# Product-key experts on one core: five dense token tiles and three gathered, with whole expert rows fetched

## The chip, the core and the metric

The kernel runs on one core of a Trainium2 chip. Its engines are TensorE (PE), VectorE (DVE), ScalarE (ACT), GpSimd (POOL) and SyncE (SP), which here only issues transfers. The metric is the time of one execution on the device in microseconds, the median of several runs.

## What is computed

One decoder layer over 1024 tokens of width 1024: normalisation, a joint projection, sliding-window and forgetting attention, a gated mix, and then the part that matters here, a product-key expert layer with 16384 experts. For each token eight heads choose 16 experts each, 128 in all:

```python
idx = jnp.take_along_axis(cidx, pos, axis=-1)         # (T, 8, 16)
g = jax.nn.softmax(top, axis=-1).astype(xc.dtype)
u = expert_down[idx]
act = jax.nn.gelu(jnp.einsum('td,thkd->thk', xc, u), approximate=False)
vv = expert_up[idx]
return jnp.einsum('thk,thkd->td', g * act, vv)
```

A last normalisation follows.

## The kernel before

The stages run one after the other: norm, projections, attention, mixing, output and second norm, `routing`, `gate_table`, `experts`. The 1024 tokens are eight tiles of 128. Every float32 product is made of three matmuls (high x high, high x low, low x high), so each weight is split by ACT (a copy, `hi`) and by DVE or POOL (a subtract, `lo`).

The expert layer is computed in two ways. For the first `DT` = 6 tiles (`SD` = 768 tokens) it is *dense*: all 16384 experts, as 128 blocks of 128, are multiplied with all tokens, and a table of gates (zero where an expert wasn't chosen) masks the result. The other two tiles (`GTILES`) are *gathered*: for each of the 128 choices ("slots") of each of these tiles an indirect DMA on POOL's queue fetches one row for each of 128 tokens. 256 slots x 2 (once the down row, once the up row) are 512 fetches of 4 KB rows, 0.5 MB each.

The down product of a dense block (gelu(down x h), L1347 to L1349 and L403 to L405) needs no gate, so it is spread over three stages: 28 blocks "ahead" in `routing`, three a head; 48 (`AHEAD_TABLE`) in `gate_table`, one a step; the other 52 (`FRESH`) in `experts`. Blocks done ahead are stored to DRAM and loaded again. Each runs in two halves of 512 and 256 tokens (`dense_cols`).

`gate_table` has 48 steps of four groups of four tokens (`GS`, `GT`). DVE builds one-hot vectors (L1869, L1873, L1890), ACT a fourth (L1943), PE multiplies them (L1830, L1831), ACT drains the group. After every four steps SP stores 4 MB of table; the load of the down block for the next step but two stands behind it in SP's queue. In between, two slots a step get their dot product on DVE (L1880, 96 in all, `TABLE_SLOTS`), from a ring of three rows.

`experts` walks over 128 chunks `c` (one expert block each). A chunk loads the up block, the gates and, if fresh, the down block, otherwise the stored gelus. DVE multiplies gate and gelu (`gate`, L2293), ACT and POOL split the weight (L2245, L2443) and the up block (L2241, L2450). PE adds up three chunks at a time (`SPAN`) for each group of 128 tokens x 512 columns (`up`, L2211 to L2213): 12 groups, four `visits` a chunk, over six PSUM banks; DVE adds each finished group to `acc` in SBUF (`add`, L2301). Between these, DVE handles the slots: first the dots of the rest of the down rows (L2308, 160), with a gelu of ACT for each 16 and a weight, then the up rows, each scaled and added to `acc` in SBUF (L2319, 256). They are dealt out by `share`, four for a fresh chunk and one for another. POOL fetches them into a ring of five rows; a fetch waits until DVE has used the buffer's last row (L2434). At the end the residual is added, the norm made and the result stored.

All order within an engine is written out by hand; engines wait for each other by semaphores.

Of the kernel before, what the change touches and what calls it, by code (L numbers as in the profile page):

```python
# [40 lines left out]
QW = 256  # L41
DT = 6
SD = DT * P
GTILES = TT - DT
# [65 lines left out]
def cols_of(x, k, h):  # L110

    return x[:, 2 * h:2 * h + 2, k]
# [1185 lines left out]
class Ahead:  # L1298


    def __init__(self, nc, m, t, a, name, first, count, raw=None, landed=None, stored=None):
        self.nc, self.m, self.t, self.a = nc, m, t, a
        self.first, self.count = first, count
        self.raw = m.at(name + "downT", [P, 2, KT, P], 172) if raw is None else raw
        self.hi = m.at(name + "downT_hi", [P, 2, KT, P], 180, F32R)
        self.lo = [m.at(name + "downT_lo0", [P, KT, P], 188, F32R), m.at(name + "downT_lo1", [P, KT, P], 15, F32R)]
# [59 lines left out]
AHEAD_TABLE = 48  # L1366
AHEAD = AHEAD_ROUTING + AHEAD_TABLE
FRESH = N_CHUNKS - AHEAD
TABLE_SLOTS = 96
# [5 lines left out]
def routing(nc, m, t, a):  # L1375
# [3 lines left out]
    ah = Ahead(nc, m, t, a, "ra_", 0, AHEAD_ROUTING, t.ra_raw, t.ra_landed)  # L1379
# [374 lines left out]
def gate_table(nc, m, t, a):  # L1754
# [3 lines left out]
    ah = Ahead(nc, m, t, a, "ga_", AHEAD_ROUTING, AHEAD_TABLE, stored=t.ga_stored)  # L1758
# [8 lines left out]
    g_hi = m.at("g_hi", [P, SD], 157, F32R)  # L1767
    g_lo = m.at("g_lo", [P, SD], 160, F32R)
    DEEP = 3
    ROWS = 3  # L1770
    LEAD = 2
    hot = [m.at(f"g_hot{i}", [P, 3, GT, P], kb, F32R) for i, kb in enumerate((192, 198, 44))]
    hot1 = [m.at(f"g_hot1_{i}", [P, GT, P], kb, BF16) for i, kb in enumerate((204, 205, 50))]
    row = [m.at(f"g_row{i}", [P, D], kb) for i, kb in enumerate((76, 80, 3))]
    r_land = [m.sem(f"g_row_landed{i}") for i in range(ROWS)]
    r_used = m.sem("g_row_used")
# [23 lines left out]
    with nc.Block() as block:  # L1800
        @block.tensor
        def _(pe):
# [8 lines left out]
            for w in range(GTILES):  # L1811
                if w:
                    pe.wait_ge(rows_copied, 2 * w)
                for k in range(KT):
                    out = m.psum[:, 2 + k // 4, (k % 4) * P:(k % 4 + 1) * P]
                    for part, x in enumerate((t.hT_hi, t.hT_lo)):
                        mm = nc.tensor.matmul(out, x[:, SD // QW, k, w * P:(w + 1) * P].bitcast(F32), t.ident[:],
                                              start=part == 0, stop=part == 1)
# [30 lines left out]
        def _(dve):  # L1849
            for x in range(6):  # L1850
                c, h = divmod(x, NH)
                dve.wait_ge(turned, x + 1)
                mine = dense_cols(h)
# [23 lines left out]
            def slot(s):  # L1877
                r = s % ROWS
                dve.wait_ge(r_land[r], (s // ROWS + 1) * 16)
                nc.vector.scalar_tensor_tensor(out=row[r][:], in0=row[r][:], scalar=1.0, in1=t.hrows[:, s // P],  # L1880
                                               op0=ALU.mult, op1=ALU.mult,
                                               accum_out=t.first_dots[:, s:s + 1]).then_inc(r_used, 1)

            def step(n, u):
                mine = range(TABLE_SLOTS * n // STEPS, TABLE_SLOTS * (n + 1) // STEPS)
                for y in range(GS):
# [6 lines left out]
                    if y == 2:  # L1893
                        ah.rest_v(dve, n + 1, 1 - u)
# [738 lines left out]
```

## Time and profile before

| | |
|---|---|
| median of 3 runs | 3502.55 us (3501.09 to 3503.83) |
| span of the profiled execution | 3503.6 us |
| PE busy | 3309.6 us, 94% |
| DVE busy | 2510.1 us, 72% |
| POOL busy | 1725.2 us, 49% |
| ACT busy | 1203.9 us, 34% |
| moved by DMA | 668.76 MB, 191 GB/s on the mean |

The profiled execution is one run, its span 1.05 us above the median of the timed ones. "L" numbers are lines of the kernel before. PE's busy time overlaps within itself (matmuls are pipelined), so its pace is read from the starts of matmuls. DMA share is the mean busy share of the core's 16 DMA engines; it can pass 1 slightly in short windows. Stages, by the first work of each: `routing` from about 970 us, `gate_table` from 1352, `experts` from 1968.

### The profile page before, as it was taken

What the parts mean: (1) busy time and instruction counts of PE and PEld (TensorE: products, weight loads), DVE (VectorE), ACT (ScalarE), POOL (GpSimd) and SP (SyncE); (2) the same over time, 40 slices, a digit from 0 to 9 for tenths busy, and PEclk for the clock granted to TensorE, in tenths of its full rate; (3) what the DMA queues carried; (4) which work ended last, traced back from release to release, by engine and by line L of the source; (5) the groups of instructions that cost most, each with busy time, mean ns of one, the idle gap of its engine ahead of it and who ended that gap; (6) DMA issues with size and microseconds to landing.
All of it is one profiled execution on the core that took longest, in us unless ns stands there. A gap on an engine that the chain in (4) does not pass through costs nothing.

```text
span 3503.6 us, 49480 instructions
## 1 busy us (share of the span) xinstructions
PE 3309.6 (94%) x17307; PEld 2817.1 (80%) x17307; DVE 2510.1 (72%) x5042; ACT 1203.9 (34%) x2314; POOL 1725.2 (49%) x1037
## 2 busy tenths in 40 slices
PE   5999988988899998999999799999999999999997
PEld 4888767777778877988888688888888888888885
DVE  5111056642469998888889588888888888888888
ACT  3111145542222223676667422222222222222222
POOL 2992000014034443111111378767877788778776
PEclk9999989999999998999999899999999999999998
DMA  5443210024222223666676688888888888888886
GB/s 205 126 128 118 72 49 13 13 91 150 78 71 92 71 69 112 251 222 243 248 255 229 250 273 265 275 253 269 273 269 268 256 274 270 273 257 264 274 260 206
DMA packets 406649, 668.76 MB, mean 191 GB/s; under 512 B 217936, under 2 KB 269208, under 8 KB 403616
## 3 DMA queue, kind: packets, MB, share of 16 engines
q1 hardware_dynamic: 325472, 371.35, 33.1%
q0 software_dynamic: 78656, 286.30, 24.9%
q10 hardware_dynamic: 2304, 8.39, 0.6%
q8 instruction: 116, 1.90, 0.2%
q14 instruction: 101, 0.83, 0.1%
HBM read 567.35 MB, written 97.55 MB: 190 GB/s over the span
## 4 chain that ended last, share of the span: by engine, by line
PE 50%; DMA 5%; DVE 5%; ACT 1%; issue 1%; SPq 0%; POOL 0%; DVEq 0%; ACTq 0%
PE psum L2211 10%; PE psum L2212 10%; PE psum L2213 10%; DMA ga_downT<-in_expert_downT 5%; PE psum L405 4%; PE psum L404 4%; PE psum L403 4%; PE psum L1347 2%; PE psum L1349 2%; PE psum L1348 2%; PE psum L1831 1%; PE psum L1830 1%; DVE g_hot L1869 1%; DVE g_hot L1890 1%; DVE g_hot L1873 1%; DVE g_row L1880 1%
## 5 line engine op out<-in xcount | busy, mean ns | idle before, releaser
L2211 PE MATMUL psum<-e_u_hi,e_w_hi 128*128 128x512 f32 x1536 | 600.0, 391 | 22.3 <-POOL e_u_lo L2450 18.6
L2212 PE MATMUL psum<-e_u_lo,e_w_hi 128*128 128x512 f32 x1536 | 599.5, 390 | 0.0
L2213 PE MATMUL psum<-e_u_hi,e_w_lo 128*128 128x512 f32 x1536 | 598.9, 390 | 0.0
L2319 DVE SCALAR_TENSOR_TENSOR acc<-e_row,e_row_weights,acc 128x1024 f32<-128x1024 f32 x256 | 481.1, 1879 | 20.4 <-DMA e_row<-in_expert_up,rows_of 12.5
L2301 DVE TENSOR_TENSOR acc<-acc,psum 128x512 f32<-128x512 f32 x508 | 337.0, 680 | 158.4 <-PE psum L2213 152.4
L2450 POOL TENSOR_TENSOR e_u_lo<-e_up,e_u_hi 128x1024 fp32r<-128x1024 f32 x128 | 385.2, 3009 | 72.1 <-ACT e_u_hi L2241 71.5
L2437 POOL DMA_INDIRECT e_row<-in_expert_up,rows_of x256 | 330.4, 1290 | 65.8 <-issue 53.4
L2211 PEld LDWEIGHTS psum<-e_u_hi,e_w_hi 128*128 128x128 f32 x1536 | 289.5, 188 | 81.8 <-issue 19.0
L2241 ACT ACTIVATE e_u_hi<-e_up 128x1024 fp32r<-128x1024 f32 x128 | 135.9, 1062 | 630.0 <-DMA e_up<-in_expert_up 410.0
L1909 POOL DMA_INDIRECT g_row<-in_expert_down,rows_of x96 | 110.8, 1154 | 485.4 <-DVE g_row L1880 467.6
L2213 PEld LDWEIGHTS psum<-e_u_hi,e_w_lo 128*128 128x128 f32 x1536 | 289.1, 188 | 60.6
L2212 PEld LDWEIGHTS psum<-e_u_lo,e_w_hi 128*128 128x128 f32 x1536 | 289.5, 189 | 58.2
L2443 POOL TENSOR_TENSOR e_w_lo<-e_table,e_w_hi 128x768 fp32r<-128x768 f32 x128 | 249.0, 1945 | 163.7 <-ACT e_w_hi L2245 162.7
L2308 DVE SCALAR_TENSOR_TENSOR e_row<-e_row,h_rows 128x1024 f32<-128x1024 f32 x160 | 275.0, 1738 | 17.2 <-DMA e_row<-in_expert_down,rows_of 17.1
L1347 PE MATMUL psum<-hT_hi,ga_downT_hi 128*128 128x512 f32 (+1 forms) x768 | 272.6, 355 | 3.7 <-DVE ga_downT_lo L1339 3.7
L405 PE MATMUL psum<-hT_hi,e_downT_lo 128*128 128x256 f32 (+1 forms) x816 | 274.2, 336 | 0.0
L404 PE MATMUL psum<-hT_lo,e_downT_hi 128*128 128x256 f32 (+1 forms) x816 | 274.2, 336 | 0.0
L403 PE MATMUL psum<-hT_hi,e_downT_hi 128*128 128x256 f32 (+1 forms) x816 | 273.9, 336 | 0.0
L495 DVE TENSOR_TENSOR pw_lo<-pw_raw,pw_hi 128x1024 fp32r<-128x1024 f32 (+1 forms) x33 | 45.5, 1378 | 316.8 <-ACT pw_hi L461 316.8
L1943 ACT ACTIVATE g_hot<-g_hot,g_lo 128x128 fp32r<-128x128 bf16 x768 | 244.5, 391 | 64.1 <-DVE g_hot L1869 61.3
L1349 PE MATMUL psum<-hT_hi,ga_downT_lo 128*128 128x512 f32 (+1 forms) x768 | 262.5, 342 | 0.0
L1348 PE MATMUL psum<-hT_lo,ga_downT_hi 128*128 128x512 f32 (+1 forms) x768 | 261.7, 341 | 0.0
(290 smaller groups left out, 7834.0 us busy)
## 6 DMA issues: line engine op xcount, KB each, us to landing
e_up<-in_expert_up SPq DMA_DIRECT2D x128, 512.0 KB
e_table<-gate_table SPq DMA_DIRECT2D x128, 384.0 KB
gate_table<-g_table SPq DMA_DIRECT2D x11, 4096.0 KB, 15.0
e_left<-gelus_ahead SPq DMA_DIRECT2D x76, 384.0 KB
e_left<-in_expert_downT SPq DMA_DIRECT2D x51, 512.0 KB
ga_downT<-in_expert_downT SPq DMA_DIRECT2D x49, 512.0 KB
gelus_ahead<-ga_gelu SPq DMA_DIRECT2D x48, 384.0 KB, 3.5
pw_raw<-in_w_in SPq DMA_DIRECT2D x34, 512.0 KB, 3.8
```

Of the source, the lines that this page charges most:

```text
L403: nc.tensor.matmul(out, l_hi(k), r_hi(k), start=k == 0, stop=False)
L404: nc.tensor.matmul(out, l_hi(k), r_lo(k), start=False, stop=False)
L405: mm = nc.tensor.matmul(out, l_lo(k), r_hi(k), start=False, stop=k == steps - 1)
L1347: mm(out, self.hi[:, u, k], dense_of(self.t.hT_hi, k, h), start=k == 0, stop=False)
L1348: mm(out, self.hi[:, u, k], dense_of(self.t.hT_lo, k, h), start=False, stop=False)
L1349: return mm(out, self.lo[u][:, k], dense_of(self.t.hT_hi, k, h), start=False, stop=k == KT - 1)
L2211: nc.tensor.matmul(to, W_hi[:, q, rows], U_hi[:, q, cols], start=c == mine[0], stop=False)
L2212: nc.tensor.matmul(to, W_hi[:, q, rows], U_lo[:, q, cols], start=False, stop=False)
L2213: mm = nc.tensor.matmul(to, W_lo[:, q, rows], U_hi[:, q, cols], start=False, stop=c == mine[-1])
L2301: nc.vector.tensor_tensor(group(j), group(j), m.psum[:, 2 + J % BANKS], ALU.add).then_inc(acc_d, 1)
L2319: nc.vector.scalar_tensor_tensor(out=mine, in0=ring[r][:], scalar=weights[:, k:k + 1], in1=mine, op0=ALU.mult, op1=ALU.add).then_inc(r_use ...
L2450: nc.gpsimd.tensor_tensor(U_lo[:, c % WRING], Uraw[:, c % 2], U_hi[:, c % WRING].bitcast(F32), ALU.subtract).then_inc(u_lo, 1)
```

## The change

Five tiles are dense (640 tokens, halves of 384 and 256) and three gathered. The tokens' tile in `hT` is 128 wide in place of 256, with high and low side by side. A new input holds for each expert its down row and its up row next to each other; a slot is one indirect DMA of 8 KB rows, 1 MB. DVE takes the dot with the first half (`dot`), ACT makes gelu and weight of this one slot (`row_weight`, two activations of 128 x 1), and DVE adds the second half, scaled, to a sum that stays in two PSUM banks for a whole tile (`add_row`), one slot later; ACT copies the sum to `acc` at the end of a tile. There are 384 slots, 40 of them in `gate_table` (one a step; that stage now has 40 steps, so 60 blocks are fresh), 344 in `experts`. The rings hold two and four 8 KB rows. The banks for groups are four; the ten groups are visited 3, 3 and 4 in turn. A fetch waits until the row sum of the slot that had its buffer is made.

```diff
-QW = 256
-DT = 6
+QW = 128
+DT = 5
 SD = DT * P
+HALVES = (0, -(-DT // 2) * P, SD)
 GTILES = TT - DT
...
 def dense_of(x, k, h):
-    return x[:, 2 * h:min(2 * h + 2, SD // QW), k]
+    return x[:, HALVES[h] // QW:HALVES[h + 1] // QW, k]

 def dense_cols(h):
-    return slice(h * HALF, min((h + 1) * HALF, SD))
+    return slice(HALVES[h], HALVES[h + 1])
...
-AHEAD_TABLE = 48
+AHEAD_TABLE = 40
...
-TABLE_SLOTS = 96
+TABLE_SLOTS = 40
+SLOTS = GTILES * P
...
-    ROWS = 3
+    ROWS = 2
...
-            def slot(s):
+            def dot(s):
                 r = s % ROWS
                 dve.wait_ge(r_land[r], (s // ROWS + 1) * 16)
-                nc.vector.scalar_tensor_tensor(out=row[r][:], in0=row[r][:], scalar=1.0, in1=t.hrows[:, s // P],
-                                               op0=ALU.mult, op1=ALU.mult,
-                                               accum_out=t.first_dots[:, s:s + 1]).then_inc(r_used, 1)
+                nc.vector.scalar_tensor_tensor(out=row[r][:, 0:D], in0=row[r][:, 0:D], scalar=1.0,
+                                               in1=t.hrows[:, s // P], op0=ALU.mult, op1=ALU.mult,
+                                               accum_out=t.dots[:, s:s + 1]).then_inc(r_dot, 1)
...
-                    for x, s in enumerate(mine):
-                        if x == y or y == GS - 1 and x > y:
-                            slot(s)
+                    if y == 1 and n < TABLE_SLOTS:
+                        dot(n)
...
+                    if y == 3 and n < TABLE_SLOTS:
+                        add_row(n)
...
             def fetch(s):
-                if s >= TABLE_SLOTS:
-                    return
-                at_least(pool, r_used, s - ROWS + 1)
-                nc.gpsimd.indirect_dma_start(out=row[s % ROWS][:], out_offset=None, in_=a.expert_down[0],
+                at_least(pool, r_acc, s - ROWS + 1)
+                nc.gpsimd.indirect_dma_start(out=row[s % ROWS][:], out_offset=None, in_=a.expert_rows,
...
-    BANKS = 6
-    RING = 5
-    SLOTS = GTILES * P
+    BANKS = 4
+    RING = 4
...
-    share = [4 if is_fresh(c) else 1 for c in range(NG)]
-    HERE = 2 * SLOTS - TABLE_SLOTS
+    share = [3 if is_fresh(c) else 1 for c in range(NG)]
+    HERE = SLOTS - TABLE_SLOTS
...
-                    to = m.psum[:, 2 + J % BANKS]
+                    to = m.psum[:, 4 + J % BANKS]
...
-            def row_gelu(e):
-                act.wait_ge(r_used, (e + 1) * TOPK - TABLE_SLOTS)
-                mine = slice(e * TOPK, (e + 1) * TOPK)
-                nc.scalar.activation(dots[:, mine], dots[:, mine], ACT.Gelu).then_inc(r_gelu, 1)
+            def row_weight(s):
+                mine = t.dots[:, s:s + 1]
+                act.wait_ge(r_dot, s - TABLE_SLOTS + 1)
+                nc.scalar.activation(mine, mine, ACT.Gelu).then_inc(r_gelu, 1)
+                act.wait_ge(r_gelu, s - TABLE_SLOTS + 1)
+                nc.scalar.activation(mine, mine, ACT.Copy, scale=t.row_gates[:, s:s + 1]).then_inc(r_weight, 1)
+                if s % P == 0:
+                    keep_sums(s // P - 1)
+
+            def keep_sums(w):
+                act.wait_ge(r_acc, (w + 1) * P - TABLE_SLOTS)
+                nc.scalar.activation(acc[:, DT + w], t.row_sums, ACT.Copy).then_inc(r_kept, 1)
...
+            def add_row(s):
+                i = s - TABLE_SLOTS
+                up_row = ring[i % RING][:, D:2 * D]
+                dve.wait_ge(r_weight, i + 1)
+                if s % P == 0:
+                    dve.wait_ge(r_kept, s // P)
+                    nc.vector.tensor_scalar(t.row_sums, up_row, t.dots[:, s:s + 1], None, ALU.mult).then_inc(r_acc, 1)
                 else:
...
+                    at_least(dve, r_acc, i)
+                    nc.vector.scalar_tensor_tensor(out=t.row_sums, in0=up_row, scalar=t.dots[:, s:s + 1],
+                                                   in1=t.row_sums, op0=ALU.mult, op1=ALU.add).then_inc(r_acc, 1)
+
+            def slot(s):
+                dot(s)
+                if s > TABLE_SLOTS:
+                    add_row(s - 1)
...
                 elif is_fresh(c):
...
+                    slot(mine[0])
+                    gate(c, 0)
+                    slot(mine[1])
+                    gate(c, 1)
+                    for s in mine[2:3]:
                         slot(s)
...
+                    for x, (J, j) in enumerate(visits(c)):
+                        add(J, j)
+                        if 3 + x < len(mine):
+                            slot(mine[3 + x])
...
-                if i >= RING:
-                    pool.wait_ge(r_used, i - RING + 1)
-                k = s % SLOTS
-                src = a.expert_down[0] if s < SLOTS else a.expert_up[0]
-                nc.gpsimd.indirect_dma_start(out=ring[i % RING][:], out_offset=None, in_=src,
-                                             in_offset=bass.IndirectOffsetOnAxis(ap=t.rows_of[:, k:k + 1], axis=0)) \
+                at_least(pool, r_acc, i - RING + 1)
+                nc.gpsimd.indirect_dma_start(out=ring[i % RING][:], out_offset=None, in_=a.expert_rows,
+                                             in_offset=bass.IndirectOffsetOnAxis(ap=t.rows_of[:, s:s + 1], axis=0)) \
                     .then_inc(r_land[i % RING], 16)
...
-        t.hT_hi = m.at("hT_hi", [P, S // QW, KT, QW], 20, F32R)
-        t.hT_lo = m.at("hT_lo", [P, S // QW, KT, QW], 52, F32R)
+        hT = m.at("hT", [P, S // QW, 2, KT, QW], 20, F32R)
+        t.hT_hi = hT[:, :, 0]
+        t.hT_lo = hT[:, :, 1]
...
+        t.row_sums = m.psum[:, 2:4].rearrange("p b n -> p (b n)")
+        t.rings = [m.at(f"e_row{i}", [P, 2 * D], kb) for i, kb in enumerate((60, 68, 76, 152))]
...
+    given["expert_rows"] = _np.concatenate([given["expert_down"][0], given["expert_up"][0]], axis=1)
```

## Rows read from the trace of the kernel before

**Rows 1.** Busy time by stage: stretch, length, engines, clock, DMA share, GB/s.

```profile
970.00:1352.00 382.00, 355.25 (x1853) 304.83 (x1851) 341.87 (x1768) 100.43 (x146) 158.39 (x51) 0.98 0.23 73
...
1968.00:2010.00 42.00, 17.67 (x65) 14.19 (x66) 15.75 (x26) 7.33 (x10) 22.12 (x16) 0.68 0.91 331
...
2010.00:3460.00 1450.00, 1450.00 (x6962) 1224.83 (x6961) 1234.36 (x1375) 338.07 (x413) 1137.21 (x658) 1.00 0.86 268
1372.00:1968.00 596.00, 583.69 (x3835) 532.21 (x3833) 511.01 (x813) 422.33 (x1100) 107.33 (x93) 0.99 0.66 234
```

**Rows 2.** Instructions in order of time, PE, experts: start, length (us).

```profile
2500.75 0.39 PE L403 MATMUL psum<-hT_hi,e_downT_hi 128*128 128x512 f32 x1
...
2506.19 0.28 PE L403 MATMUL psum<-hT_hi,e_downT_hi 128*128 128x256 f32 x1
...
2509.06 0.40 PE L2211 MATMUL psum<-e_u_hi,e_w_hi 128*128 128x512 f32 x1
```

**Rows 3.** The same, PE, gate table.

```profile
1622.13 0.22 PE L1830 MATMUL psum<-g_hot 128*128 128x128 f32 x1
...
1622.97 0.45 PE L1347 MATMUL psum<-hT_hi,ga_downT_hi 128*128 128x512 f32 x1
```

**Rows 4.** Chain of waits that ended last, in order of time: start, us, what.

```profile
1361.61 3.85 PE psum L1817 x32
...
1421.46 0.66 SPq L1986
...
1422.17 16.94 DMA ga_downT<-in_expert_downT
...
1441.45 0.60 DVE g_hot L1869
...
1445.06 1.14 DVE g_row L1880 x2
...
1450.96 1.14 DVE ga_downT_lo L1339
...
1821.00 0.63 SPq L1986
...
1977.54 19.54 DMA e_table<-gate_table
...
2009.07 0.76 PE psum L2211
...
3494.59 3.68 DVE e_row L2356 x3
```

**Rows 5.** Who waited for whom, routing, then steady experts: total us, times, longest.

```profile
DVE r_best L1589 <- PE psum L1493: 33.5, 2, 17.3
...
DVE acc L2301 <- PE psum L2213: 149.8, 148, 1.4
...
DVE e_row L2308 <- DMA e_row<-in_expert_down,rows_of: 8.6, 11, 1.3
```

**Rows 6.** Instructions in order of time, DVE and POOL, experts.

```profile
2504.30 2.74 POOL L2450 TENSOR_TENSOR e_u_lo<-e_up,e_u_hi 128x1024 fp32r<-128x1024 f32 x1 [2.37 <-ACT e_u_hi L2241]
...
2504.71 3.41 DVE L2308 SCALAR_TENSOR_TENSOR e_row<-e_row,h_rows 128x1024 f32<-128x1024 f32 x1
```

**Rows 7.** Groups: busy us, mean ns; then one by tile: ns min/median/max.

```profile
L2319 DVE SCALAR_TENSOR_TENSOR acc<-e_row,e_row_weights,acc 128x1024 f32<-128x1024 f32 x256 | 481.1, 1879 | 20.4 <-DMA e_row<-in_expert_up,rows_of 12.5
...
L2308 DVE SCALAR_TENSOR_TENSOR e_row<-e_row,h_rows 128x1024 f32<-128x1024 f32 x160 | 275.0, 1738 | 17.2 <-DMA e_row<-in_expert_down,rows_of 17.1
...
L2301 DVE TENSOR_TENSOR acc<-acc,psum x508: 671/680/689, 2035.4 to 3481.1; 128x512 f32<-128x512 f32 x170
```

**Rows 8.** Busy time in three stretches with full DMA engines, columns as above.

```profile
35.00:40.00 5.00, 3.65 (x18) 3.56 (x18) 3.10 (x8) 4.35 (x7) 0.00 (x0) 1.00 1.04 362
10.00:25.00 15.00, 0.00 (x0) 0.00 (x0) 14.00 (x13) 0.00 (x0) 0.00 (x0) 1.00 1.01 425
1974.00:1998.00 24.00, 12.74 (x55) 10.20 (x53) 7.36 (x12) 4.99 (x6) 13.37 (x12) 0.78 1.02 382
```

More of the change, by code:

```diff
@@ L1816, in _ @@
                     for part, x in enumerate((t.hT_hi, t.hT_lo)):
-                        mm = nc.tensor.matmul(out, x[:, SD // QW, k, w * P:(w + 1) * P].bitcast(F32), t.ident[:],
-                                              start=part == 0, stop=part == 1)
+                        tile = x[:, DT + w, k]
+                        mm = nc.tensor.matmul(out, tile.bitcast(F32), t.ident[:], start=part == 0, stop=part == 1)
                     if k % 4 == 3:
@@ L1913, in _ @@
             pool.wait_ge(rows_made, 2 * GTILES)
-            fetch(0)
-            fetch(1)
-            pool.wait_ge(gate_kept, 16)
-            fetch(2)
-            def step(n, u):
-                for s in range(TABLE_SLOTS * n // STEPS, TABLE_SLOTS * (n + 1) // STEPS):
-                    fetch(s + ROWS)
-            for n in range(STEPS):
-                step(n, n % 2)
+            for s in range(TABLE_SLOTS):
+                fetch(s)
         @block.scalar
@@ L2245, in weight_high, with gelus @@
                 nc.scalar.activation(W_hi[:, c % WRING], Gc[:, c % 2], ACT.Copy).then_inc(w_hi, 1)
-            nc.scalar.activation(dots[:, 0:TABLE_SLOTS], t.first_dots[:, 0:TABLE_SLOTS], ACT.Gelu) \
-                .then_inc(r_gelu, TABLE_SLOTS // TOPK)
+            def gelus(f, h):
+                act.wait_ge(a_done, f * 2 + (h + 1))
+                if f:
+                    act.wait_ge(mul, 2 * fresh_at[f - 1] + (h + 1))
+                cols = dense_cols(h)
+                nc.scalar.activation(Wg[:, cols], m.psum[:, h, 0:cols.stop - cols.start], ACT.Gelu).then_inc(gelu, 1)
+            act.wait_ge(t.table_stored[1], 16 * (SD // TABLE_TOKENS // 2))
             for c in range(NG):
-                for e in units_over(c):
-                    row_gelu(e)
+                mine = slots(c)
+                up_high(c)
                 if is_fresh(c):
                     f = fresh_no(c)
-                    up_high(c)
-                    for h in range(NH):
-                        act.wait_ge(a_done, f * 2 + (h + 1))
-                        if f:
-                            act.wait_ge(mul, 2 * fresh_at[f - 1] + (h + 1))
-                        cols = dense_cols(h)
-                        nc.scalar.activation(Wg[:, cols], m.psum[:, h, 0:cols.stop - cols.start], ACT.Gelu) \
-                            .then_inc(gelu, 1)
+                    early = 0 if c == 0 else 1
+                    for s in mine[0:early]:
+                        row_weight(s)
+                    gelus(f, 0)
+                    for s in mine[early:2 * early]:
+                        row_weight(s)
+                    gelus(f, 1)
                     weight_high(c)
+                    for s in mine[2 * early:]:
+                        row_weight(s)
                     if f + 1 < FRESH:
@@ L2476, in _ @@
                     rest_u(c)
-                    for s in mine:
-                        fetch(s)
+                    refill(mine)
             pool.wait_ge(gate2_land, 16)
```

243 lines of the change are left out of this document (115 added, 128 removed).

## The prediction

> **What bounds the kernel now.** I read the page's busy shares first and then went stage by stage through the windows, since an average over stages with different limits says little. Three stages change in length. Routing (970 to 1352 us): PE 355 of 382 us, DVE 342. Gate table (1372 to 1968): PE 584 of 596, DVE 511. Experts, steady part (2010 to 3460): PE 1450 of 1450, DVE 1234, POOL 1137, DMA share 0.86 at 268 GB/s [rows 1]. A busy PE is not yet a PE at its peak, so I worked out its pace. From the first to the last of 24 matmuls with 512 columns lie 5.44 us, 0.227 us each; the 24 of 256 columns take 2.87 us, 0.120 each [rows 2]. The PE work of the experts stage, in full flow from 2009.1 us [rows 4], is 4608 x 0.227 = 1045 us for the up products and 51 x 24 x (0.227 + 0.120) = 425 us for the fresh down products: 1470 us, and nothing of it can be left out: PE has no idle time in the windows, and DVE waits for it, 150 us in total before its adds of a group [rows 5]. So this part runs at PE's pace.
>
> In the gate table the pace is set twice. Eight one-hot matmuls take 0.84 us [rows 3], so a step of 32 of them with 24 + 24 matmuls of the down product is 11.7 us of PE, 47 a block of four steps. The chain of waits also shows a loop: the 4 MB table store goes out, the next expert block is queued behind it on SP and lands 16.9 us later, ACT and DVE split it, DVE works through some 28 us more, and the next store goes out. From the store at 1421.46 to that at 1821.00 are eight blocks, 49.9 us each [rows 4].
>
> **The change, part by part.** *One dense token tile less.* All 128 expert blocks now have 640 columns, cut 384 + 256. A matmul of 384 columns I put halfway between the two measured ones, 0.173 us (between 0.120 and 0.227). It streams three or four segments of 128 where it had two of 256; a product with one contiguous segment (L2211, 0.40) and one with two (L403, 0.39) last the same [rows 2], so segments cost nothing here, and a few per cent of PE's work at worst.
>
> Routing: 28 blocks save 24 x 0.054 = 1.3 us each on PE, 36 us in all. But DVE carries this stage: it waited for PE only twice, 33.5 us in total [rows 5], once at the start and once after the three blocks of the first head. Only the second wait shrinks, by 3 x 1.3: **-4 us**, bounds 0 and -10.
>
> Gate table: 40 steps, not 48, thus ten blocks and not twelve. A DVE step had 12 TensorTensors at 0.60, two dots of a row at 1.14 and one rest of the down block at 1.14 [rows 4], 10.6 us; now one dot and one add-row take the place of two dots, the same. Bytes in a block stay (one 8 KB fetch for two of 4 KB). PE falls to 10.4 us a step, but the loop through SP keeps all its members, so I keep 49.9 us a block: **-100 us**. If the loop gives way and DVE's four steps (43 us) set the block, up to 70 us more go. The stage's head has a third token tile to turn back, 3.85 us of PE before its copy [rows 4]: **+4**. The fetch ring has two buffers, not three: the next fetch goes out after the add-row at a step's end and has a step, 11 us, to land; its POOL queue holds nothing else.
>
> Experts, start (1968 to 2010, DMA share 0.91 [rows 1]): POOL issues 4 + 3 fetches of 1.05 MB in place of ten of 0.52, 2.1 MB more; at 382 GB/s [rows 8] that is **+5 us**. The tail keeps its form: 0.
>
> Experts, steady. *PE*: 10 groups, not 12: 3840 x 0.227 = 871; fresh blocks are 60 now, 59 of them here: 59 x 24 x (0.173 + 0.120) = 414. Together **1285 us**, 185 less.
>
> *DVE*: 344 slots, each one dot and one add-row, 688 instructions where 416 stood. Without a collision a dot takes 1.14 us to the next start [rows 4]. The add-row reads SBUF and PSUM and writes PSUM, which no row shows at 1024 elements: three of the same operation over SBUF took 3.68 us, 1.23 each and the last one's tail with it [rows 4], and an add with a PSUM operand took 0.68 for 512 [rows 7]. I take 1.20, bounds 1.14 (the dot) and 1.36 (two adds). Sum: dots 344 x 1.14 = 392; add-rows 413; group adds 433 x 0.60 = 260; gates 128 x 0.60 x 640/512 = 96; rests of the down block 59 x 1.14 = 67: 1228 us. To this come collisions. A dot that began at 2504.71 while POOL's subtract ran from 2504.30 took 3.41 us [rows 6]. The means are 1.74 us over 160 dots and 1.88 over 256 adds [rows 7]; alone they would last 1.22 and 1.28 (the above, and the 0.08 by which neighbours overlap), which makes 83 + 154, some 235 us. The adds from PSUM kept to 671 to 689 ns, all 508 [rows 7]. So what reads two SBUF tiles is held for as long as POOL's instruction runs and what reads one is not. Only the 344 dots can collide now, and behind each stands a PSUM operation of 1.2 us in which POOL gets through half its subtract. I take half, 118 us, bounds 60 and 235: **1346 us**.
>
> Did add-rows wait as the adds of now do, they would cost 154 / 256 x 344 = 207 us more, and DVE's floor would be 1553. The Trainium skill ("SBUF — State Buffer", Who interferes with whom) describes the port pair of DVE and GpSimd as an exclusive lock, wanted by a DVE instruction with two SBUF inputs; by it alone the add-row, with one, never waits. No row here shows an operation with one SBUF and one PSUM input other than the group adds, which agree.
>
> *DMA*: 344 x 1.05 = 361 MB of rows (218 before), up blocks 67, table 42, kept gelus 22, down blocks 31: **523 MB** against 390. At 268 GB/s for a share of 0.86 (312 at 1) that would be 1676 us. In stretches where the engines were full they moved more: 382 GB/s with 256-byte table pieces and 4 KB rows mixed (1974 to 1998 us, share 1.02), 425 with rows of 8 KB and 4 KB from DRAM (10 to 25 us, share 1.01) [rows 8]. The mix of the first is nearest, also in its share of small pieces: 523 / 0.382 = **1369 us**; bounds 1231 and 1676.
>
> The three floors thus lie at 1285, 1346 and 1369, and none is far enough ahead of the others to run without gaps: fetches wait for add-rows, add-rows for ACT (two small activations behind the copy of the up block, which itself waits for its transfer), PE for four banks and not six. In the gate table PE needs 48 x 11.7 = 562 us and the stretch lasts 596, 6% more; in the steady part of now, with one engine well ahead, it is 0%. I take 5%: 1369 x 1.05 = 1437, **-33 us** against 1470. What hides each edit: ACT's 688 new small instructions lie in its idle time (338 busy of 1450 [rows 1]); if one waits behind a late up block, DVE stalls with it, and that is in the 5%.
>
> **Sum.** Profiled span 3503.6; -4, -100, +4, +5, -33 = -128: 3375.6. The median of the runs is 1.05 us below the profiled span, so 3374.5.
>
> **Rivals.** (a) DMA becomes the bound and is slow. Rows of 8 KB from random places, with table pieces of 256 bytes taking turns against them, stay at the 312 GB/s of today's steady part: 1676 us, +206 instead of -33, 3614 us, slower. It decides from where the steady part takes 1573 us, a rate of 333 GB/s. For it: 268 GB/s at 0.86; the second table block took 19.5 us to land when the start was crowded [rows 4]. Against: 382 at a share of 1.02 [rows 8], so the share overstates how full they are. Chance 0.12.
> (b) DVE with all of its collisions: 1228 + 235 = 1463, and 5%: 1536, 3474 us. For it: POOL's instructions keep their number. Against: fewer instructions that can collide. Chance 0.17.
> (c) Reads of DRAM as a whole are capped, not the engines' packets: from 35 to 40 us the engines were full at 362 GB/s [rows 8]. 523 / 0.362 = 1445, and 4%: 1503, 3441 us. Against: 425 GB/s came from DRAM just before [rows 8], though not from random rows. Chance 0.10. The Trainium skill states a limit of memory of about 358 GB/s for a core ("DMA: Bandwidth & Descriptors", Specifications); the 425 of the trace lies above it, and by the page's figure the steady part could not fall under an estimated 523 / 0.358 = 1461 us.
> (d) PE still binds, and the gate table's loop loosens: 1285 x 1.02 = 1311 and blocks of 45 us: 126 and 49 us less than the forecast, 3200. With one of the two: 3250 to 3330. For it: today PE hides everything at 0.86. Chance 0.13.
> (e) The change does less than it says: a row of 8 KB goes as two packets of 4 KB, so that fetching costs per byte what it does now. The rate of the mixed stretch already is one with 4 KB rows, so this changes the time by little.
>
> **How the numbers follow.** The forecast (3340 to 3430, steady part 1400 to 1495) has 0.48, (a) 0.12, (b) 0.17, (c) 0.10, (d) 0.13. The range for 8 in 10 leaves out most of (a) and the lower half of (d): 3280 to 3520. Differences under 0.2% can't be told here. Faster by over 0.2% (below 3495.5): all but (a) and an edge of (b), 0.86; same 0.02; slower 0.12.
>
> **What would show it.** Ten table stores some 50 us apart (44 would be (d)). Routing within 5 us of 382. In the steady part DMA above 0.95 at 360 to 385 GB/s and DVE at 93% or more; PE between 88 and 92%, waiting for banks or weights, where now it never waits. Waits of dots for fetches of 50 us and more (now 8.6, over 11 of them [rows 5]). Add-rows at 1.2 to 1.3 us with a maximum near that; one that reached 3 us would refute the port argument. The prediction is wrong if the rate at full share stays under 333 GB/s, or if DVE's add-row costs more than 1.5 us.

## The result, and the profile after

The changed kernel takes **3537.5 us** (median of 5 runs, 3519.5 to 3544.3) against 3503.6 us before: 1.0095 times as long, 95% interval 1.0071 to 1.0119. It is slower, by about 1%; the forecast was 3374.5, with a range up to 3520. The profiled execution is the quickest of the five (span 3517.7 us): beside the profile of before it shows 14 of the 34 us between the medians. One of the six runs of kernel 2 below took 10,500 us at a granted clock of 0.46 and is in no ratio; its profile too is of its quickest run (3476.4 us).

The experts' steady part, columns as in [rows 1]:

```profile
1910.00:3465.00 1555.00, 1358.13 (x6535) 1150.60 (x6533) 1371.20 (x1736) 481.19 (x1103) 967.69 (x586) 0.95 0.94 329
```

Routing lasts 372.8 us, 9.5 less, and the last table store goes out 92 us sooner, counted from routing's end (524 us, 616 before). All of that and more goes in the experts stage, which lasts 1651 us and not 1536. In its steady part no engine is busy throughout: PE 1358 of 1555 us, where before it was 1450 of 1450; DVE 1371; DMA 0.94 at 329 GB/s. DVE's busy time and its waits make up the whole of the stretch (1371 and 184 us), so it is DVE that sets the pace, by its work and by what it waits for. With gaps in its work PE's granted clock is 0.95 of 2.4 GHz in the mean, where it was 1.00.

Who waited for whom in the steady part (total us, times, longest); SP's row is its instruction queue standing still:

```profile
DVE e_row L2336 <- DMA e_table<-gate_table: 130.9, 48, 5.2
DVE e_row L2336 <- DMA e_row<-in_expert_rows,rows_of: 49.0, 34, 3.9
...
SPq L2141 <- DVE e_downT_lo L2314: 1124.7, 57, 22.8
```

SP's issues in order of time (start, length, line, what):

```profile
2521.54 0.53 SPq L2159 DMA_DIRECT2D e_table<-gate_table  x1
2540.45 0.33 SPq L2141 DMA_DIRECT2D e_left<-in_expert_downT  x1
2540.83 0.43 SPq L2154 DMA_DIRECT2D e_up<-in_expert_rows  x1
```

From 2522.1 to 2540.5, for 18 us, SP stands in the wait of `load_down` for DVE's rest of the last down block, and the up rows and gates of the next chunk are queued behind it. The queue stood there in the kernel before, too (2010 to 3460 us):

```profile
SPq L2128 <- DVE e_downT_lo L2285: 760.7, 50, 19.7
```

But now `landed(c)` comes ahead of the first slot of a fresh chunk, where three slots stood ahead of it, and DVE pays: its dot at 2524.78 us had waited 3.5 us for these gates.

The rows of dots and add-rows (whole kernel), with DMA packets of 1910 to 3465 us behind them:

```profile
L2336 DVE SCALAR_TENSOR_TENSOR e_row<-e_row,h_rows 128x1024 f32<-128x1024 f32 x344 | 543.3, 1579 | 192.3 <-DMA e_table<-gate_table 130.9
...
L2349 DVE SCALAR_TENSOR_TENSOR psum<-e_row,row_dots,psum 128x1024 f32<-128x1024 f32 x342 | 437.5, 1279 | 0.0
...
DMA packets 246335, 511.99 MB, mean 329 GB/s; under 512 B 171366, under 2 KB 171366, under 8 KB 203241
```

The add-row and the collisions of the dot are as forecast (1279 ns; 344 x (1579 - 1226) = 121 us, with 1226 ns the median of the dots). So three questions stand: what SP's order costs, what rate the DMA engines reach, and where the floors of DVE and PE lie.

### The profile page after: what moved, and what is told of

Its sections match the earlier page's. It is cut to its first block, busy times and chain, and to the rows that moved or that the text cites. A ratio compares the mean times of both kernels' runs of the same rounds, so it can differ in the third digit from the quotient of the medians.

```text
span 3517.7 us, 48087 instructions
## 1 busy us (share of the span) xinstructions
PE 3061.9 (87%) x16312; PEld 2662.7 (76%) x16312; DVE 2569.2 (73%) x5232; ACT 1285.4 (37%) x2916; POOL 1606.9 (46%) x908
## 4 chain that ended last, share of the span: by engine, by line
DVE 24%; DMA 22%; issue 8%; POOL 4%; ACT 2%; PE 1%; SPq 1%; DVEq 0%; ACTq 0%; POOLq 0%
DMA e_table<-gate_table 9%; DMA e_row<-in_expert_rows,rows_of 8%; DVE psum L2349 7%; DVE e_row L2336 5%; DMA ga_downT<-in_expert_downT 4%; POOL e_u_lo L2468 2%; DVE acc L2330 2%; DVE g_hot L1875 2%; DVE g_hot L1905 2%; POOL e_w_lo L2461 2%; DVE e_table L2322 2%; DVE g_hot L1879 1%; DVE ga_downT_lo L1340 1%; DVE e_downT_lo L2314 1%; DVE psum L1897 1%
## 5 line engine op out<-in xcount | busy, mean ns | idle before, releaser
L2336 DVE SCALAR_TENSOR_TENSOR e_row<-e_row,h_rows 128x1024 f32<-128x1024 f32 x344 | 543.3, 1579 | 192.3 <-DMA e_table<-gate_table 130.9
L2455 POOL DMA_INDIRECT e_row<-in_expert_rows,rows_of x344 | 375.9, 1093 | 396.5 <-DVE psum L2349 360.1
L2224 PE MATMUL psum<-e_u_lo,e_w_hi 128*128 128x512 f32 x1280 | 524.6, 410 | 0.0
L2225 PE MATMUL psum<-e_u_hi,e_w_lo 128*128 128x512 f32 x1280 | 522.8, 408 | 0.0
L2349 DVE SCALAR_TENSOR_TENSOR psum<-e_row,row_dots,psum 128x1024 f32<-128x1024 f32 x342 | 437.5, 1279 | 0.0
L1925 POOL DMA_INDIRECT e_row<-in_expert_rows,rows_of x40 | 164.7, 4119 | 338.3 <-DVE psum L1897 306.6
L404 PE MATMUL psum<-hT,e_downT_hi 128*128 128x256 f32 (+1 forms) x944 | 295.6, 313 | 25.9 <-DVE e_downT_lo L2314 25.8
L406 PE MATMUL psum<-hT,e_downT_lo 128*128 128x256 f32 (+1 forms) x944 | 294.1, 312 | 0.0
L405 PE MATMUL psum<-hT,e_downT_hi 128*128 128x256 f32 (+1 forms) x944 | 293.8, 311 | 0.0
L2461 POOL TENSOR_TENSOR e_w_lo<-e_table,e_w_hi 128x640 fp32r<-128x640 f32 x128 | 219.6, 1715 | 114.6 <-ACT e_w_hi L2265 113.4
L404 PE MATMUL psum<-hT,pw_hi 128*128 128x512 f32 (+1 forms) x544 | 212.4, 390 | 3.8 <-DVE pw_lo L496 2.1
L1348 PE MATMUL psum<-hT,ga_downT_hi 128*128 128x384 f32 (+1 forms) x640 | 212.2, 332 | 3.5 <-DVE ga_downT_lo L1340 3.5
L405 PE MATMUL psum<-hT,pw_hi 128*128 128x512 f32 (+1 forms) x544 | 212.3, 390 | 0.0
```

The source lines that it names most:

```text
L404: nc.tensor.matmul(out, l_hi(k), r_hi(k), start=k == 0, stop=False)
L405: nc.tensor.matmul(out, l_hi(k), r_lo(k), start=False, stop=False)
L406: mm = nc.tensor.matmul(out, l_lo(k), r_hi(k), start=False, stop=k == steps - 1)
L2224: nc.tensor.matmul(to, W_hi[:, q, rows], U_lo[:, q, cols], start=False, stop=False)
L2225: mm = nc.tensor.matmul(to, W_lo[:, q, rows], U_hi[:, q, cols], start=False, stop=c == mine[-1])
L2336: nc.vector.scalar_tensor_tensor(out=ring[r][:, 0:D], in0=ring[r][:, 0:D], scalar=1.0, in1=t.hrows[:, s // P], op0=ALU.mult, op1=ALU.mult, ...
```

## The experiments

Each kernel is the changed one with the edit shown. Before was timed beside them, at 3502 to 3505 us. Kernels 1, 2, 3 and 11 leave nothing out; the others have two runs each, which lie 1 to 10 us apart.

**1. The wait moved back.**

```
-                landed(c)
+                if not is_fresh(c) or c == 0:
+                    landed(c)
...
                     slot(mine[0])
+                    landed(c)
                     gate(c, 0)
```

> Only the place of one wait differs: DVE's wait for the chunk's table stands behind the first slot of a fresh chunk instead of ahead of it. In the changed kernel the steady part of the experts stage lasts 1555 us, of which DVE is busy 1371, waits 131 for the table and 49 for rows; the DMA engines show a share of 0.94 at 329 GB/s. Theory A (a late start: SP issues the table's load late, and the wait stands ahead of work that doesn't need it): the first dot and add-row, 2.4 us, now cover most of the 48 waits of 2.7 us on the mean; 60 to 110 us less, 3420 to 3470. Theory B (throughput: the engines can't move more than about 350 GB/s, a floor of 1462 us): the wait only changes its name, from the table to rows; under 20 us less.

3502.2 us, 0.9993 of before (0.9983 to 1.0003). The waits of dots for gates are gone, and 35 us with them, which is neither the 60 to 110 of theory A nor B's under 20. 70 us (in 1910 to 3200) have moved to DVE's gates, which now wait for ACT, and the waits for rows went from 40 to 70.

**2. SP's order.** The down block of the next fresh chunk is issued after the next chunk's up rows and gates.

```
+                if is_fresh(c) and fresh_no(c) + 1 < FRESH:
+                    load_down(fresh_no(c) + 1)
                 if c + 1 < NG and not is_fresh(c + 1):
                     load_gelu(c + 1)
-                elif c + 1 < NG and fresh_no(c + 1) + 1 < FRESH:
-                    load_down(fresh_no(c + 1) + 1)
```

> Only SP's order differs: the load of the next fresh down block, which waits until DVE is done with the last one (SP waited there 1125 us in the steady part), stands behind the up and table loads of the next chunk instead of ahead of them. Theory A: table and up block are issued up to 19 us earlier, DVE's 131 us of waits for the table go, and what is left is DVE's 1371 us and some waits for rows: 90 to 140 us less, 3390 to 3440. Theory B (throughput): under 20 us less, the waits show up at rows.

3488.7 us, 0.9954 (0.994 to 0.9967): 49 us of the 163 by which the forecast missed, and a little faster than before. Theory A had promised 90 to 140 us. Below are its steady part (a shorter stretch, in which all kernels are in full flow) and two groups:

```profile
1910.00:3200.00 1290.00, 1154.31 (x5641) 980.66 (x5640) 1204.22 (x1478) 406.06 (x947) 806.48 (x499) 0.96 0.95 339
...
L2336 DVE SCALAR_TENSOR_TENSOR e_row<-e_row,h_rows 128x1024 f32<-128x1024 f32 x290 | 468.8, 1617 | 83.2 <-DMA e_row<-in_expert_rows,rows_of 80.4 <-DMA e_table<-gate_table 1.8
...
L2322 DVE TENSOR_TENSOR e_table<-e_gelu,e_table 128x384 f32<-128x384 f32 x105 | 103.5, 986 | 3.6 <-ACT e_gelu L2272 3.5
```

The gates of fresh chunks now take 986 ns in the mean, longest 2571, where the changed kernel has 786 and 1570 (1910 to 3200 us). They too read two SBUF tiles and fall on POOL's subtract: part of the cure is given back as collisions. DVE is busy for 1204 us and waits for 86 of the 1290, most of it (80) for rows. Of the chain of waits that ended last 34% are row fetches and 10% POOL's subtract, as from 2528.3 us on: a subtract of 2.75 us, the fetch that stands behind it in POOL's order, issued at 2531.2 though its add-row had ended 1.2 us before, and 8.8 us until that row lands.

**3. Both.**

> Both orders at once: SyncE issues the next fresh block's down rows after the next chunk's up rows and gates (3488.7 us by itself) and VectorE waits for the gates behind the first slot of a fresh chunk (3502.2 by itself). If both cure one and the same wait, as I hold, the two gains do not add: within 8 us of 3489. The rival, that they cure different waits (together some 80 us off 3537): 3465 or less.

3484.2 us, 0.9944 (0.9927 to 0.996), no different from 2 within the intervals. The two cure one wait. What is left above the forecast, 110 us, lies elsewhere.

**4. No row fetches.** All fetches but the first four are left out, and the dots multiply by 0 (so dots and sums are not the right ones), in SP's order as changed:

```
                 i = s - TABLE_SLOTS
+                if i >= RING:
+                    return
...
-                dve.wait_ge(r_land[r], (i // RING + 1) * 16)
+                dve.wait_ge(r_land[r], 16)
```

> Leaves out, in the experts stage, every fetch of rows but the first four, and multiplies the dots by zero; all work of DVE, ACT and PE stays. The floor of DVE with its collisions, without DMA: the steady part falls from 1555 to 1380 to 1430 (DVE busy 1371 of it), 3345 to 3395 in all, by theory A and B alike. If DVE were busy beyond 97% and the time within 20 us of DVE's busy sum, DVE is the next bound. If the collisions with POOL came partly from POOL's issuing of fetches, the dots' mean of 1579 ns falls too.

3421.0 us, above the expected 3345 to 3395, with DMA at a share of 0.37. Even with two thirds of the bytes gone, dots wait 68 us for gates (1910 to 3200; 116 in the changed kernel), so more than half of those waits need no full DMA engines: they come from SP's order.

**5. Dots and add-rows on 16 columns**, all fetches kept: DVE's work falls to less than half, and what binds is the DMA engines.

```
-                nc.vector.scalar_tensor_tensor(out=ring[r][:, 0:D], in0=ring[r][:, 0:D], scalar=1.0,
-                                               in1=t.hrows[:, s // P], ...
+                nc.vector.scalar_tensor_tensor(out=ring[r][:, 0:16], in0=ring[r][:, 0:16], scalar=1.0,
+                                               in1=t.hrows[:, s // P, 0:16], ...
```

> Leaves out, in the experts stage, most of the slots' arithmetic: dots and add-rows take 16 columns in place of 1024 (some 0.1 to 0.2 us each instead of 1.2); all fetches and waits stay. It shows the floor of DMA and PE without DVE. Theory B (throughput): the steady part can't fall under 512 MB at 350 GB/s, 1462 us, so 3420 to 3450 in all, at a share of 0.98 and more. Theory A: DMA can do more once loads are asked for early; the rate passes 360 GB/s and the steady part comes to 1300 to 1420 us, 3260 to 3380.

3435.9 us. This is the floor of the DMA engines (DVE 565 of 1290 us, share 0.98 at 350 GB/s), and it lies 61 us above the forecast of the whole kernel. SP's order is still the late one here; kernel 10's second variant has the early one and comes to 3424.7 us with the engines as full (0.98 at 352), so the late order may account for some 11 us of this floor. Two more kernels ask why the rate is 350 and not 382. The second row is the first of these.

```profile
1910.00:3200.00 1290.00, 1176.33 (x5807) 1011.63 (x5808) 565.36 (x1528) 416.91 (x978) 713.63 (x515) 0.96 0.98 350
```

```profile
1910.00:3200.00 1290.00, 1209.73 (x6107) 1042.88 (x6107) 618.27 (x1611) 437.13 (x1031) 756.66 (x543) 0.99 0.96 368
```

**6. The same with gates from a contiguous block** (`sp.dma_start(Gc[:, c % 2], t.gelus[c % AHEAD])`; the gates are then not the right ones).

> The changed kernel with VectorE's dots and add-rows on 16 columns (as in the narrow kernel, 3435.9 us, DMA share 0.98 at 350 GB/s), and with each expert chunk's gates loaded from a contiguous block of 327 KB (2.5 KB a row) and not as 256-byte pieces of the gate table; left out are therefore the full dot products, the up rows' sum and the right gates. Theory S (the small pieces cost the DMA engines their rate): the rate at full share rises from 350 to 385 GB/s or more, and the time falls by 80 us or more, to about 3350, where TensorE's work (1285 us of the stretch and its waits) takes over. Rival M (the rate is a cap of the memory side, whatever the pieces): still 345 to 360 GB/s and within 15 us of 3436.

3351.3 us, 85 us less, for the same number of bytes. The pieces of 256 bytes, 69% of all packets but 8% of the bytes, cost that. 368 GB/s at a share of 0.96 is 383 at 1. The Trainium skill ("DMA: Bandwidth & Descriptors", Specifications) says that a transfer needs pieces of 512 bytes or more for the full rate, with which this run agrees (256 bytes against 2.5 KB; no run tries a size between). It also gives about 358 GB/s as memory's limit for a core, its half of a stack; 1290 us at a mean of 368 lie above that. So neither this limit nor the 362 GB/s of rival (c) is what held the rate at 350.

**7. The same as 5 with rows in sequence** (`nc.gpsimd.dma_start(out=ring[i % RING][:], in_=a.expert_rows[k * P:(k + 1) * P])`, not by index; the rows are then not the right ones).

> The narrow kernel again (16 columns), its gate table as in the changed kernel, but each slot's 128 rows of 8 KB fetched as one contiguous block of expert_rows by an ordinary DMA on GpSimd's queue, not by index; left out are the full dot products, the sum, and the right rows. Theory G (rows gathered at random cost more than rows in sequence; the head of the kernel moved sequential rows at 425 GB/s): the rate rises above 385 GB/s and the time falls by 60 us or more below the narrow kernel's 3436. Rival M (the cap is on all traffic): 345 to 360 GB/s and within 15 us of 3436.

3426.8 us, 352 GB/s at a share of 0.98. The 9 us less are within the spread: kernel 5's own two runs lie 10 us apart. That rows of 8 KB come from random places costs next to nothing.

**8. The floor of DVE.** SP's order of 2 and no row fetches.

> Early order (3488.7) and no row fetched in the experts stage but the first four; left out are the right dot products and sums. The rows' traffic is gone and VectorE keeps all of its work. Theory V (VectorE and its collisions are the floor, the rows' waits of 80 us in 1290 come from too little slack behind it): the time falls by those waits at most, 3400 to 3440, and VectorE is busy over 97% of 1910 to 3200 us. Rival P (TensorE's waits for banks and weights are a bound of their own): VectorE stays at 94% or less.

3345.9 us. DVE is busy 1287 of 1290 us:

```profile
1910.00:3200.00 1290.00, 1216.13 (x6149) 1043.07 (x6148) 1287.06 (x1613) 442.80 (x1033) 520.94 (x228) 0.99 0.39 114
...
L2336 DVE SCALAR_TENSOR_TENSOR e_row<-e_row,h_rows 128x1024 f32<-128x1024 f32 x316 | 548.1, 1735 | 0.0
...
L2322 DVE TENSOR_TENSOR e_table<-e_gelu,e_table 128x384 f32<-128x384 f32 x114 | 54.5, 478 | 2.9 <-ACT e_gelu L2272 2.9
```

It fell by more than I had expected (3400 to 3440). Beside the rows' waits the collisions of the gates went, 986 to 478 ns: with fetches, POOL waits for an add-row before 169 of 290 (367 us of 1290 in kernel 2), so its subtracts start where DVE goes on to a dot or a gate. That last step is read from the order of the code and was not tested by itself.

**9. The floor of PE.** As 8, with dots and add-rows on 16 columns.

> Early order, no row fetched in the experts stage but the first four, dots and add-rows on 16 columns; left out are the dot products and the sum of up rows. DMA traffic and VectorE's work are both out of the way, so this shows TensorE's floor, which I worked out as 1285 us for the steady part: 3489 less 200 to 240 us, 3250 to 3290. If it stays above 3320, TensorE's own work was mis-sized (its 384-column matmuls, four banks and not six, or the clock).

3219.6 us, PE 1277 of 1290 us busy at a clock of 1.00. My expectation (3250 to 3290) was too high. The forecast's own 1285 us for PE in place of the 1437 give 3374.5 - 152 = 3222.5.

**10. Which floor holds the kernel with SP's order mended?** Gates from a contiguous block, all of DVE's work kept:

> Early order (3488.7), dots and add-rows in full, with each chunk's gates loaded from a contiguous block and not as 256-byte pieces; left out are the right gates. Theory D (with SyncE's order mended the steady part is held by the DMA engines, and their rate by the small pieces): 3430 to 3460, and VectorE's waits for rows fall from 88 us to under 30. Rival V (VectorE's 1297 busy of 1390 us is the tighter floor, the pieces cost only where it has slack): within 15 us of 3489.

3475.1 us, 14 less than in 2 (0.9917 of before, 0.9897 to 0.9937): the small pieces, 85 us where DVE has slack, cost little here. Theory D, which I held, had promised 3430 to 3460 and waits for rows under 30 us. These stay at 79 us, though the DMA engines are down to a share of 0.92:

```profile
1910.00:3200.00 1290.00, 1153.35 (x5656) 981.76 (x5655) 1206.33 (x1480) 406.49 (x947) 813.15 (x501) 0.96 0.92 340
...
DVE e_row L2335 <- DMA e_row<-in_expert_rows,rows_of: 79.3, 80, 2.8
```

The waits for rows in kernel 2 are therefore hardly the price of a low rate. The chain of kernel 2, and the same chain here (31% row fetches, 10% POOL's subtract), points at when a fetch goes out and how long it takes: 7.7 us to land in the median, with a ring of four buffers. That is read from the traces; a deeper ring, or fetches ahead of subtracts on POOL, was not tried.

And no collisions for the dots, by multiplying with the sum in PSUM (`in1=t.row_sums`, with two waits of DVE on its own last results, before which it stands still for some 30 us in 1290; the dot products are not the right ones):

> Early order, but the dot multiplies the row with the sum in PSUM and not with the token rows in SBUF; left out is the right dot product. The port argument: an operation with one SBUF and one PSUM input is never held by GpSimd, so the dot's maximum falls from over 4 us to under 1.4 and VectorE's busy time in the steady part by some 110 us. Theory D (DMA holds the steady part now): the time falls by less than 25 us, the rest goes into waits for rows. Rival V (VectorE is the floor): 60 us or more, 3430 or less.

3424.7 us, 64 less. All 301 dots took 1206 to 1224 ns, and DVE's busy time fell by 87 us (110 expected):

```profile
L2337 DVE SCALAR_TENSOR_TENSOR e_row<-e_row,psum x301: 1206/1214/1224, 1911.1 to 3197.5; 128x1024 f32<-128x1024 f32 x151
...
1910.00:3200.00 1290.00, 1178.21 (x5858) 1004.28 (x5857) 1117.66 (x1534) 422.40 (x983) 727.03 (x517) 0.97 0.98 352
```

DVE is therefore the tighter bound in 2 (rival V, in both kernels), and with the collisions gone the DMA engines are full (0.98 at 352 GB/s) and bind. Both edits together:

> Early order, the dot against the sum in PSUM (no collisions; 3424.7 by itself) and gates from contiguous blocks (3475.1 by itself); left out are the right dots and gates. If the two floors lie close behind each other, as I hold, the second cure is worth more once the first is made: 3355 to 3395, 30 us or more below 3424.7. If the small pieces cost only the 14 us that they cost alone, 3405 to 3415.

3393.0 us. The contiguous gates, worth 14 us alone, are worth 32 now: the two floors lie one behind the other. The dots' collisions are worth 64 us and 82.

**11. The gate table's loop.** SP's order of 2, and the 4 MB store of a block in two halves (by experts 0 to 63 and 64 to 127), the second behind the next load of a down block; the waits on the stores count 32 a block.

```
+                if q % BS == 0 and n:
+                    ...
+                    sp.dma_start(half, out[:, 1 - buf, P // 2:P]).then_inc(stored[1 - buf], 16)
                 ah.store(sp, n, u)
...
-                        sp.dma_start(t.table[:, words], out[:, buf].rearrange("p e c -> p (e c)")) \
+                        sp.dma_start(half, out[:, buf, 0:P // 2]).then_inc(stored[buf], 16)
```

> The early order of SyncE's loads (3488.7) with the gate table's store of 4 MB a block cut into two halves of 2 MB, the second issued behind the next step's load of down rows. Theory L (each block of the gate table is 50.6 us and not 43 to 45 because that step's down rows land 18 us after their issue, behind the store): the landing falls below 12 us, blocks take 46 to 48 us, and the kernel gains 25 to 50 us: 3440 to 3465. Rival (the loop is bound by the bytes of the block, or by its engines, 448 and 430 of 503 us busy): blocks stay within 0.7 us of 50.6 and the time within 8 us of 3489.

**3437.8 us**, 0.9811 of before (0.9795 to 0.9828), a complete kernel. ACT's wait for down blocks from 1363 to 1820 us in the changed kernel, then SP's issues and the same wait in this one:

```profile
L1331 ACT ACTIVATE ga_downT_hi<-ga_downT 128x1024 fp32r<-128x1024 f32 x37 | 39.2, 1059 | 73.0 <-DMA ga_downT<-in_expert_downT 70.2
```

```profile
1406.07 1.69 SPq L2008 DMA_DIRECT2D gate_table<-g_table  x1
1407.81 0.43 SPq L1320 DMA_DIRECT2D ga_downT<-in_expert_downT  x1
1408.28 0.89 SPq L1996 DMA_DIRECT2D gate_table<-g_table  x1
...
L1331 ACT ACTIVATE ga_downT_hi<-ga_downT 128x1024 fp32r<-128x1024 f32 x40 | 42.4, 1060 | 28.8 <-DMA ga_downT<-in_expert_downT 25.9
```

A block takes 45.6 us, where the changed kernel takes 50.6, and ten of them are the gain of 51 (at the edge of the 25 to 50 expected). The down blocks behind the store had landed 18 to 20 us after their issue. With the late wait of 1 added:

> Early order of SyncE's loads, late wait of VectorE for the gates, and the table's store in two halves, all three, complete. The first two cure the same wait (3484.2 together, 3488.7 for the first alone), the third is worth 51 us by itself: 3432, within 8 us. That is about 2% under the kernel before. If the halves had worked through the experts' start and not the gate table's loop, the late wait would take the same gain again: 3437 to 3440, no better than without it.

3437.9 us, the same: the late wait adds nothing that shows once SP's order is mended. The time lies within 8 us of the expected 3432 and in the rival's 3437 to 3440 as well, so it doesn't tell the two apart; the stores 45.6 us apart, here too, do.

## Why the prediction was wrong

The floors can now be set beside those of the forecast, each as a time of the whole kernel (the forecast's sum without its 5% is 3374.5 - 68 = 3306.5 us with the DMA floor of 1369, and goes with the other floors in its place):

| floor | forecast | measured | kernel |
|---|---|---|---|
| PE | 3222.5 (1285 us) | 3219.6 | 9 |
| DVE with collisions | 3283.5 (1346) | 3345.9 | 8 |
| DMA | 3306.5 (1369) | 3435.9 | 5 |

The term that failed is that of the steady part, 1369 x 1.05 = 1437 us. Its floor was too low, its 5% was too small for how the engines hold each other up, and a wait was put at nothing. The miss is 163 us.

**The rate of the DMA engines** was taken as 382 GB/s, from 24 us at the stage's start [rows 8]. Measured at full engines it is 350: 523 / 0.350 = 1494 us, 125 more than 1369, and the floor came out 129 higher (118 with SP's early order). With the forecast's own 5% this alone makes 1569 us and 3506 in all, no gain. I had called that stretch the nearest because of its mix, and in pieces of under 512 bytes it is indeed like the steady part (66% of its packets, 69% there). What it has besides, and the steady part has not, is two stores of the gate table, 3.4 of its 9.2 MB; whether these lifted the rate was not tested. A share of 1.02 also says that so short a stretch is not measured well. The other end, 312 GB/s, came from engines at 0.86; the truth lay between, and I took the short stretch as the value.

**But the rate alone is not what holds the kernel up.** Kernel 10's first variant has SP's order mended and the small pieces gone, with which the engines reach 383 GB/s at a share of 1 (kernel 6), the rate of the forecast. It still takes 3475.1 us, 101 above the forecast, and gains only 14 on kernel 2. The second step that failed is therefore **the overlap, 5% or 68 us, for floors lying close**. That kernel 2 is 53 us above its highest floor looks as if the size were right, but this is luck: kernel 10 lies 124 us above its own highest floor (3351.3 in kernel 6, which has the late order still; DVE 3345.9). What stands in its place is DVE's chain. In kernel 2 DVE is busy for 1204 and waits for 86 of 1290 us; for 344 slots (290 of them in this stretch) that is 1530 us, where the forecast has 1437 in all and 1346 of work. By the same measure the dots' collisions are 134 us (forecast 118), those of the gates, which were not counted, some 60 (120 x (986 - 478) ns), and the waits some 100: with 1346 and the 16 us by which the dots exceed their forecast this makes some 1520. Without the dots' collisions the kernel is 64 us faster, without these and the small pieces 96 (3393.0).

**The third is a wait that the forecast did not see.** It counted the instructions moved and not the wait moved: `landed(c)` stands ahead of all slots of a fresh chunk, with SP's queue late by up to 22.8 us behind `load_down`. The changed kernel is 49 us above kernel 2, which cures it. It was readable in the trace of before (SP stood in the same wait) together with the diff.

The prices are not independent and can't be added up to the miss: the small pieces cost 85 us, 14 or 32, according to what else is cured. What a deeper ring or another order on POOL would do to the waits for rows stays open.

**DVE** was right in the dot, the add-row (1.20 to the next start, as forecast) and the changed kernel's collisions (121 us, forecast 118). As a floor it is 62 us too low: with DVE never idle the dots take 1735 ns, 344 x (1735 - 1220) = 177 us of collisions, which are 59 of the 62. The gates don't collide in that kernel (478 ns), but do in kernel 2 (986). The port argument holds: add-rows 1276 to 1291 ns in kernel 2, dots with a PSUM operand 1224 at most, while dots with two SBUF inputs reached 4155 in the changed kernel. The Trainium skill ("SBUF — State Buffer", Who interferes with whom) says so for one SBUF input and for two, and the gates of kernel 2, with two, agree (2571 ns at the longest).

**Routing** gained 9.5 us where 4 were forecast, inside its bounds. **The gate table**: ten stores 50.6 us apart (49.9 forecast), 92 us gained for 96; its loop is what the chain said, and kernel 11 shows the price of its member on SP, 5 us a block. **PE** was right to 3 us. It had to wait for banks and weights as forecast, and was 87% busy in the steady part, where 88 to 92 were forecast.

**The signs of being wrong** that the prediction named did not come: the add-row is far from 1.5 us, and the rate at full share is above 333 GB/s. That limit was worked out from a steady part of 1573 us without the 5% that the forecast itself adds. With it the change breaks even at 523 / (1573 / 1.05) = 349 GB/s, and 350 is what was measured.

**The rivals.** (a) set the point of change at 333 GB/s; the mean was 329 at a share of 0.94, and the kernel is slower, but the engines themselves reach 350 and 49 us of the miss are SP's order. (c) put the rate at 362 GB/s and its floor 49 us below the measured 1494, for a reason that kernel 6 excludes. (b) is the nearest once SP's order is mended: 1536 us of steady part and 3474 in all against 1530 and 3488.7 in kernel 2, though by another division: it had 235 us of collisions and 73 of allowance, and there were some 195 of collisions and 100 of waits. (d) is right in that the gate table's loop can come down to 45 us a block, but only with the store cut in two. (e) did not happen: 43,094 of the 246,335 packets have 8 KB or more, about 128 for each of the 336 fetches of the steady part, so a row goes as one packet. That DVE's chain, the rate and the moved wait come together was in no rival. The chance of 0.12 for slower was too small, and the range ended 17 us too low.

## What to carry to other kernels

When a change brings the work of several engines up to one level, every small wait that the one bound engine used to hide is paid: follow each wait that the diff moves to what is queued ahead of it on the issuing queue. A rate for a long stretch is to be taken from a long stretch of the same traffic, and where only full engines for 24 us and ones at 0.86 for 1450 us are there, neither is the value. A floor says what an engine could do alone; when floors lie within some per cent of each other, follow the loop through ring, fetch, dot and add-row as well, since here a rate mended by itself gained 14 us of 3489. Cut work with a PSUM operand from the count of collisions, and put every instruction with two SBUF inputs into it, the short ones too.

## What the runs showed of the hardware

- Pieces of 256 bytes hold back large rows on the same DMA engines: 350 GB/s at 0.98 with them, 368 at 0.96 without, for 8% of the bytes (kernels 5 and 6).
- Rows of 8 KB fetched by index and rows in sequence move at 350 and 352 GB/s (kernels 5 and 7).
- The dot of 1024 elements with one SBUF and one PSUM input takes 1206 to 1224 ns with POOL at work, as fast as with two SBUF inputs and no collision (1206 at the least in kernel 8). The add-row, which writes PSUM as well, took 1273 to 1292 (changed kernel, kernels 1 and 2).
- POOL's subtract of 1024 elements is held by the collisions too: 2379 to 2439 ns in kernel 10's second variant, where no dot collides; 3379 in the median in the changed kernel and 2770 in kernel 2, 3476 at most (1910 to 3200 us).
- A load of 0.5 MB behind a 4 MB store in SP's queue landed 18 to 20 us after its issue; with the store cut in two and one half behind the load, ACT's waits for such loads fell from 70 to 26 us in 457 (kernel 11).
